# A transformer front on one core: input loaded token-major, turned and scaled by a matmul with a diagonal, and a new order of transfers and small work

## The chip, the cores and the metric

The kernel runs on one core of a Trainium2 chip. The metric is device time in microseconds of one execution, lower is better. The engines named here: TensorE (PE, matmuls), VectorE (DVE), ScalarE (ACT), GpSimd (POOL), SyncE (SP, which issues the transfers).

## The reference

Two transformer-like layers in sequence over 512 tokens of width 1024, in float32. The change concerns only the beginning of the first one:

```
mod = silu(c) @ w_ada + b_ada            # 6144 numbers: sh1, sc1, ga1, sh2, sc2, ga2
y   = x * rsqrt(mean(x * x, -1) + EPS)   # a root of each token
xn  = (y * g_mix) * (1 + sc1) + sh1
proj = xn @ w_in + b_in                  # q, k, v, index q, index k, index weights, RNN inputs, gates
score = sum_h wi[q,h] * relu(qi . ki)    # for the choice of the 128 best keys of a query
```

From `proj` come an attention over the chosen keys, a gated linear recurrence (RG-LRU) behind a causal convolution, a merge, a feed-forward part, and then a second layer with 16 meta tokens ahead. The recurrence needs `softplus(-lam)` of 1024 numbers, called the factor below.

## The kernel before

Everything is held with features on the partitions: `H` is [128, 8, 528], eight chunks of 128 features by 16 meta tokens and 512 tokens. Weights come in 560 units of 512 KB, each [128, 8, 128], through two buffers `raw`. GpSimd splits each unit into a high and a low part (`Whi`, `Wlo`, L422 to L428); TensorE multiplies the split input by the split weight with three matmuls for each chunk (L443 to L445), 24 for a unit over 512 tokens. A split waits until TensorE has left the slot (`half_done`, `unit_done`), and SyncE loads a unit when the unit two before it has been split (`weights_ready`).

The engines run one list of instructions each and are ordered by semaphores alone. The front, in the order of its lists:

SyncE loads c, part of the constants, two small tables for the bias rows (`REL`, `OH`), x already transposed into `H` in four transfers of 512 KB, the meta tokens, the vectors `V`; then the rows of `w_ada`, 512 KB each, into eight slots `AW`: 16 rows in the order of `FRONT_ROWS` (scale and shift of each chunk), and 24 more. A row waits until the row eight before it has been used (`ada_done`). `UNIT_BEHIND_ROW` and `AHEAD` say behind which rows the weight units 0 to 11 are issued; a unit that waits holds everything behind it.

ScalarE squares the chunks of x (L966), TensorE sums them over the partitions with a matrix of 1/1024 (L525), ScalarE makes the roots `RSTP`. VectorE reduces each row against silu(c) to one number per partition (L1391), multiplies x by the roots two chunks at a time (`spread`, L1395), and ScalarE applies scale and shift twice, to the high half `XAhi` (L982) and to the plain product `NTP` in PSUM (L985); VectorE takes the difference as `XAlo` (`low(k)`, L1400). Units 0 to 3 are multiplied chunk by chunk as these arrive (`BLOCKS`): the groups hold 1, 3, 4, 4, 5, 5, 5 and 5 blocks of three matmuls. VectorE takes the first four pairs of rows before the first spread.

Behind the front VectorE's list holds the 16 rows L1369 (`modulation`), with `bound_ratio` (four small instructions) after eight of them; then `WI`, the index weights (L1475, `wi_ready`), for which the score matmul n == 3 waits; then 24 score sums with the last eight rows between them; then the factor, 28 small instructions (`factor_begin`, `factor_terms`, `factor_end`, L1435 to L1467); then the products for the meta tokens (L1539) and the taps of the first convolution (L1547), for which the first gate matmuls (L586) wait. TensorE runs units 4, 5 and 6, the transposes for `WI`, six scores (L557) behind each of units 6 to 9, and the recurrence units from 10 on, with the first gates behind unit 13. Some matmuls on zeros (L514, L531) fill TensorE's time at the start.

Of the kernel before, what the change touches and what calls it, by code (L numbers as in the profile page):

```python
# [75 lines left out]
UNIT_BEHIND_ROW = {3: 0, 5: 1, 8: 2, 10: 3}  # L76
AHEAD = {2: 4, 4: 5, 14: 6, 17: 7, 19: 8, 21: 9, 23: 10, 24: 11}
# [43 lines left out]
def build(nc, xT, metaT, vecs, rel, onehot, consts, crow, ada, gatew, units, scratch, out):  # L121
    with ExitStack() as ctx:
        def sb(name, shape, dt=F32, frame=ctx):
            return frame.enter_context(nc.sbuf_tensor(name, shape, dt))

        def sem(name):
            return ctx.enter_context(nc.semaphore(name))
# [34 lines left out]
        sb("fill", [P, 40])  # L162
# [5 lines left out]
        RSTP = A45[:, 0:S]  # L168
        NTP = [A45[:, 0:512] if k in (5, 7) else A45[:, 512:1024] for k in range(KC)]
# [5 lines left out]
        with ExitStack() as f:  # L175
# [6 lines left out]
            XS = RG8  # L182
# [78 lines left out]
        v_in, xs_ready, meta_copied = sem("v_in"), sem("xs_ready"), sem("meta_copied")  # L261
# [88 lines left out]
        def _(sp):  # L350
            sp.dma_start(CR[0:1, :], crow.rearrange("(o d) -> o d", o=1)).then_inc(c_in, 16)
            sp.dma_start(CON[:, 0:C_ONE], consts[:, 0:C_ONE]).then_inc(mean_in, 16)
            sp.dma_start(REL[:, :], rel).then_inc(small_in, 16)
            sp.dma_start(OH[:, :], onehot).then_inc(small_in, 16)
            for j in range(KC // 2):
                sp.dma_start(H[:, 2 * j:2 * j + 2, META:T], xT[:, 2 * j:2 * j + 2, :]).then_inc(x_in[j], 16)
                if j == 0:
                    sp.dma_start(H[:, :, 0:META], metaT).then_inc(meta_in, 16)
                if j == 1:
                    sp.dma_start(V[:, :], vecs).then_inc(v_in, 16)  # L360
# [79 lines left out]
        def _(pe):  # L440
# [89 lines left out]
            for _ in range(11):  # L530
                pe.matmul(gp[0][:, 0:HALF], SQS[:, 0:P], SQS[:, 0:HALF], start=True, stop=True)  # L531
# [3 lines left out]
            for j, blocks in enumerate(BLOCKS):  # L535
                pe.wait_ge(xn_ready, j + 1)
                for u, k in blocks:
                    if (u, k) == (1, 0):
                        pe.wait_ge(rb_copied, 1)
                    if (u, k) == (2, 0):  # L540
                        pe.wait_ge(meta_copied, 1)
                    split_wait(u, k)
                    mm = three(gp[u % 2][:, (u // 2) * 512:(u // 2) * 512 + S], u, k, XAhi[:, k, :], XAlo[:, k, :], k == 0, k == KC - 1)
                    if k == KC // 2 - 1:
                        mm.then_inc(half_done, 1)
                    if k == KC - 1:
                        mm.then_inc(unit_done, 1)
# [362 lines left out]
        def _(act):  # L910
# [51 lines left out]
            for k in range(KC):  # L962
                act.wait_ge(x_in[k // 2], 16)
                if k >= 2:
                    act.wait_ge(stat_mm, k - 1)
                act.activation(sq[:, k % 2, 0:S], H[:, k, META:T], ACT.Square).then_inc(sq_ready, 1)  # L966
                if k == KC // 2:
                    act.wait_ge(meta_in, 16)
                    act.activation(MSQ[:, :, :], H[:, :, 0:META], ACT.Square).then_inc(meta_sq, 1)
            act.wait_ge(stat_mm, KC)  # L970
            inverse_root(RSTP, RSTP, EPSC, rstd_ready)
# [289 lines left out]
        def _(dve):  # L1261
# [123 lines left out]
            dve.wait_ge(silu_c, 1)  # L1385

            def rows(k):
                for n, c in ((2 * k, KC + k), (2 * k + 1, k)):
                    w = AW[n % ADA_SLOTS]
                    dve.wait_ge(ada_in[n % ADA_SLOTS], 16 * (n // ADA_SLOTS + 1))  # L1390
                    dve.tensor_tensor_reduce(w[:, :], w[:, :], CSP, 1.0, 0.0, ALU.mult, ALU.add, MOD[:, c:c + 1]).then_inc(ada_done, 1)  # L1391
                dve.drain().then_inc(mod_ready, 1)
# [15 lines left out]
            spread(2)
            low(1)
            spread(3)  # L1410
            low(2)
            rows(4)
            low(3)
            rows(5)
            low(4)
            rows(6)
            rows(7)
            for k in (5, 6, 7):
                low(k)
# [51 lines left out]
            modulation(ADA_FIRST + 8, ADA_FIRST + 16)  # L1471
# [172 lines left out]
            dve.drain()  # L1644
            residual(1, U_OUT, 1, 2 * KC)
# [329 lines left out]
```

## Time and profile before

| | us |
|---|---|
| median of 3 runs | 1746.54 (1746.23 to 1747.31) |
| the profiled execution, its own time | 1745.25 |
| its span in the profile | 1743.3 |
| TensorE busy | 1714.8 (98%) |
| GpSimd busy | 1473.8 (85%) |
| VectorE busy | 1080.4 (62%) |
| ScalarE busy | 530.5 (30%) |

Times in the trace are microseconds from the start of the span; durations marked ns are nanoseconds. Busy time of TensorE is that of its pipelined matmuls, so neighbours overlap; the granted clock (PEclk) is a share of full speed, where 1.00 is 2.4 GHz and 0.50 is 1.2 GHz. An idle time stands in brackets with the instruction that ended it.

### The profile page before, as it was taken

The numbers are of one execution on the slowest core, as the hardware profiler recorded it, in microseconds if no ns is written. First come the engines' busy times: TensorE is split into PE (matmuls) and PEld (weight loads), VectorE is DVE, ScalarE is ACT, GpSimd is POOL, SyncE is SP. The second block draws the span as 40 slices with busy tenths as digits, with TensorE's granted clock in tenths as the row PEclk, the third lists the DMA queues.
The fourth block names the chain that finished last, engine by engine and source line by source line (L and its number), as shares of the span: only waits on it lengthen the run. The fifth ranks groups of instructions, "written<-read, shape, count | busy, mean of one in ns | idle before, by whom it ended". The sixth has DMA issues, their size and how long they took to land.

```text
span 1743.3 us, 35057 instructions
## 1 busy us (share of the span) xinstructions
PE 1714.8 (98%) x12334; PEld 1531.0 (88%) x12334; DVE 1080.4 (62%) x1682; ACT 530.5 (30%) x801; POOL 1473.8 (85%) x2245
## 2 busy tenths in 40 slices
PE   8999999999999999999999999999999999999998
PEld 5667776678899999988899999999999999999887
DVE  6788998845566767622678676876685455555102
ACT  5336664311221211100443444444343211111001
POOL 4577996578999999999689888988897999999885
PEclk8999999999999999999999999999999999999999
DMA  9942332232332332333222222222232332333332
GB/s 341 394 143 82 94 100 89 93 107 87 98 96 86 94 95 86 97 109 108 62 86 84 86 73 86 86 76 83 80 92 73 97 93 88 96 96 96 97 108 97
DMA packets 55384, 184.54 MB, mean 106 GB/s; under 512 B 6721, under 2 KB 9953, under 8 KB 55298
## 3 DMA queue, kind: packets, MB, share of 16 engines
q1 hardware_dynamic: 52066, 177.53, 32.2%
q10 hardware_dynamic: 3232, 5.77, 0.9%
q8 instruction: 66, 1.08, 0.3%
q14 instruction: 20, 0.16, 0.0%
HBM read 178.56 MB, written 4.72 MB: 105 GB/s over the span
## 4 chain that ended last, share of the span: by engine, by line
PE 90%; DVE 5%; DMA 1%; ACT 1%; DVEq 1%; issue 1%; SPq 1%; ACTq 0%; POOL 0%; POOLq 0%
PE gp L443 28%; PE gp L444 28%; PE gp L445 28%; DMA AW<-ada 1%; PE A L586 1%; DMA raw<-units 1%; PE A L804 1%; PE A L619 1%; PE gp L645 1%; PE A L855 1%; PE A L637 0%; DVE AW L1391 0%; PE A L799 0%; PE A L857 0%; PE A L847 0%
## 5 line engine op out<-in xcount | busy, mean ns | idle before, releaser
L426 POOL TENSOR_TENSOR Wlo<-raw,Whi 128x256 fp32r<-128x256 f32 x1120 | 981.0, 896 | 46.7
L443 PE MATMUL gp<-XNhi,Whi 128*128 128x258 f32 (+3 forms) x2736 | 840.1, 307 | 8.1 <-DVE XNlo L1400 3.2
L444 PE MATMUL gp<-XNlo,Whi 128*128 128x258 f32 (+3 forms) x2736 | 829.4, 303 | 0.0
L445 PE MATMUL gp<-XNhi,Wlo 128*128 128x258 f32 (+3 forms) x2736 | 827.0, 302 | 0.0
L443 PEld LDWEIGHTS gp<-XNhi,Whi 128*128 128x128 f32 x2736 | 515.4, 188 | 41.4 <-issue 11.9
L444 PEld LDWEIGHTS gp<-XNlo,Whi 128*128 128x128 f32 x2736 | 515.6, 188 | 23.5 <-issue 2.4
L445 PEld LDWEIGHTS gp<-XNhi,Wlo 128*128 128x128 f32 x2736 | 515.0, 188 | 22.0
L422 POOL TENSOR_TENSOR probe<-raw 1x1 f32<-1x1 f32 x560 | 180.6, 323 | 203.9 <-PE gp L445 140.2
L423 POOL TENSOR_SCALAR Whi<-raw 128x512 fp32r<-128x512 f32 x560 | 342.5, 612 | 0.0
L443 PE MATMUL gp<-AChi,Whi 128*128 128x512 f32 (+1 forms) x374 | 141.0, 377 | 0.0
L444 PE MATMUL gp<-AClo,Whi 128*128 128x512 f32 (+1 forms) x374 | 140.8, 377 | 0.0
L445 PE MATMUL gp<-AChi,Wlo 128*128 128x512 f32 (+1 forms) x374 | 140.8, 377 | 0.0
L443 PEld LDWEIGHTS gp<-AChi,Whi 128*128 128x128 f32 x374 | 70.4, 188 | 13.0
L445 PEld LDWEIGHTS gp<-AChi,Wlo 128*128 128x128 f32 x374 | 70.4, 188 | 13.0
L444 PEld LDWEIGHTS gp<-AClo,Whi 128*128 128x128 f32 x374 | 70.4, 188 | 12.7
L930 ACT ACTIVATE sq<-H 128x512 f32<-128x512 f32 (+1 forms) x24 | 15.2, 633 | 180.2 <-DVE H L1305 147.7
L1303 DVE TENSOR_TENSOR H<-gp,H 128x514 f32<-128x514 f32 (+2 forms) x15 | 10.4, 693 | 94.4 <-PE gp L445 94.2
L1242 ACT ACTIVATE ffn_val<-ZZ,V 128x512 f32<-128x512 f32 x22 | 18.0, 817 | 154.6 <-DVEq L1843 154.6
L1846 DVE SCALAR_TENSOR_TENSOR ffn_val<-ZZ,V,ffn_val 128x512 f32<-128x512 f32 x44 | 43.9, 998 | 31.6 <-ACT ffn_val L1242 27.9
L1305 DVE SCALAR_TENSOR_TENSOR H<-gp,MOD,H 128x512 f32<-128x512 f32 (+1 forms) x16 | 12.0, 751 | 82.6 <-PE gp L445 82.2
L1723 DVE TENSOR_TENSOR DD<-h_G 128x640 f32<-128x640 f32 x48 | 56.1, 1182 | 5.7 <-issue 1.2
L1741 DVE TENSOR_TENSOR XX<-h_k,EE 128x320 f32<-128x320 f32 x48 | 49.4, 1028 | 0.0
(334 smaller groups left out, 2234.9 us busy)
## 6 DMA issues: line engine op xcount, KB each, us to landing
raw<-units SPq DMA_DIRECT2D x280, 512.0 KB, 3.5
AW<-ada SPq DMA_DIRECT2D x40, 512.0 KB, 8.5
AWL<-ada SPq DMA_DIRECT2D x8, 512.0 KB, 3.6
bias_rows<-RB ACTq DMA_DIRECT2D x1, 2560.0 KB, 19.8
H<-xT SPq DMA_DIRECT2D x4, 512.0 KB, 6.6
BIAS<-bias_rows ACTq DMA_DIRECT2D x1, 2048.0 KB, 7.8
out<-H SPq DMA_DIRECT2D x8, 256.0 KB, 2.2
WG<-gatew ACTq DMA_DIRECT2D x8, 128.0 KB, 2.0
```

The costliest lines, as they stand in the source:

```text
L422: pool.tensor_tensor(probe[0:1, 0:1], src[0:1, c0:c0 + 1], src[0:1, c0:c0 + 1], ALU.add)
L423: pool.tensor_scalar(hi[:, c0:c1], src[:, c0:c1], 1.0, 1.0, ALU.mult, ALU.mult).then_inc(hi_made, 1)
L426: ins = pool.tensor_tensor(lo[:, c:c + UNIT // 4], src[:, c:c + UNIT // 4], hi[:, c:c + UNIT // 4].bitcast(F32), ALU.subtract)
L443: pe.matmul(dst, Whi[s][:, k, :], rhi, start=start, stop=False)
L444: pe.matmul(dst, Whi[s][:, k, :], rlo, start=False, stop=False)
L445: return pe.matmul(dst, Wlo[s][:, k, :], rhi, start=False, stop=stop)
L586: pe.matmul(A45[:, r * 512:(r + 1) * 512], WG[:, r * P:(r + 1) * P], XC[b % 2][:, :], start=True, stop=True).then_inc(gate_mm, 1)
L619: pe.matmul(A45[:, g * 512:g * 512 + (i + 1) * P], Q[g * HD:(g + 1) * HD, r * 2 + e, i * P:(i + 1) * P], K[g * HD:(g + 1) * HD, 0:(i + 1) ...
L1242: act.activation(YV[:, :], ZZ[:, 0, 2:2 + S], ACT.Identity, bias=fw(3), scale=fw(2)).then_inc(ya_first, 1)
L1723: dve.tensor_tensor(DD[:, l % 2, :].rearrange("p (j t) -> p j t", t=2 * b), g, g[:, :, b - 1:b].to_broadcast([P, TP // (2 * b), 2 * b]), A ...
L1741: dve.tensor_tensor(x[:, :, 0, :], k[:, :, 0, :], e[:, :, 0, :], ALU.mult)
L1846: dve.scalar_tensor_tensor(YV[:, :], ZZ[:, 0, tap:tap + S], V[:, bass.ds(VEC["ffn2"] + i * 4 + tap, 1)], YV[:, :], ALU.mult, ALU.add)
```

## The change

x is loaded twice: first with tokens on the partitions, four transfers of 512 KB into `XK`, and once more transposed into `H`, in one transfer of 2 MB behind the last row of `w_ada`, for the residual much later. The two small tables go behind x. VectorE sums the squares of a token along its row, one reduction for each 128 tokens (`TOK`); ScalarE makes 512 roots as [128, 4]; VectorE scales the identity by them (`DIAG`). A matmul of a 128x128 piece of `XK` with the diagonal turns the piece and scales it (`turned(k)`: four for each chunk, into the PSUM bank `XSP`), in place of the sums over partitions and of `spread`. ScalarE's two passes read `XSP`, and `NTP` is one bank instead of two. VectorE's rows and low halves alternate: row 2k, low k-1, row 2k+1. Units 0 and 1 are issued two rows earlier, units 6 to 11 one to six rows earlier. The factor moves from behind the scores to between the 16 modulation rows ahead of `WI`.

```diff
-UNIT_BEHIND_ROW = {3: 0, 5: 1, 8: 2, 10: 3}
-AHEAD = {2: 4, 4: 5, 14: 6, 17: 7, 19: 8, 21: 9, 23: 10, 24: 11}
+UNIT_BEHIND_ROW = {1: 0, 3: 1, 8: 2, 10: 3}
+AHEAD = {2: 4, 4: 5, 8: 6, 11: 7, 14: 8, 17: 9, 20: 10, 23: 11}
...
+        XSP, NTP = A45[:, 0:S], A45[:, S:2 * S]
+        DIAG = sq[:, 0, 0:S].rearrange("p (t n) -> p t n", t=QT)
...
+            XK = RG8[:, :, :].rearrange("p k n -> p (k n)").rearrange("p (t d) -> p t d", t=QT)
... SyncE
+            for t in range(QT):
+                sp.dma_start(XK[:, t, :], xrow[t, :, :]).then_inc(x_in[t], 16)
+                if t == 0:
+                    sp.dma_start(H[:, :, 0:META], metaT).then_inc(meta_in, 16)
+                if t == 2:
+                    sp.dma_start(V[:, :], vecs).then_inc(v_in, 16)
             sp.dma_start(REL[:, :], rel).then_inc(small_in, 16)
             sp.dma_start(OH[:, :], onehot).then_inc(small_in, 16)
...
+            sp.dma_start(H[:, :, META:T], xT).then_inc(h_in, 16)
             load_units(U_RNN + 2, U_ROUT)
... TensorE
-            for k in range(KC):
-                pe.wait_ge(sq_ready, k + 1)
-                pe.matmul(RSTP, mean, sq[:, k % 2, 0:S], start=(k == 0), stop=(k == KC - 1)).then_inc(stat_mm, 1)
...
-            for _ in range(11):
+            def turned(k):
+                if k:
+                    pe.wait_ge(nt_ready, k)
+                for t in range(QT):
+                    mm = pe.matmul(XSP[:, t * P:(t + 1) * P], XK[:, t, k * P:(k + 1) * P], DIAG[:, t, :], start=True, stop=True)
+                mm.then_inc(xs_mm, 1)
+            for _ in range(4):
+                pe.matmul(gp[0][:, 0:HALF], SQS[:, 0:P], SQS[:, 0:HALF], start=True, stop=True)
+            pe.wait_ge(diag_ready, 1)
+            turned(0)
+            for _ in range(6):
                 pe.matmul(gp[0][:, 0:HALF], SQS[:, 0:P], SQS[:, 0:HALF], start=True, stop=True)
...
             for j, blocks in enumerate(BLOCKS):
+                if j + 1 < KC:
+                    turned(j + 1)
                 pe.wait_ge(xn_ready, j + 1)
... ScalarE
+            act.wait_ge(tok_sums, 1)
+            act.activation(TOK[:, 1, :], TOK[:, 0, :], ACT.Ln, bias=EPSC, scale=1.0 / D)
+            act.drain()
+            act.activation(TOK[:, 1, :], TOK[:, 1, :], ACT.Exp, scale=-0.5).then_inc(rstd_ready, 1)
...
-                act.wait_ge(xs_ready, k // 2 + 1 if k != 5 else KC // 2)
-                act.activation(XAhi[:, k, :], XS[:, k, :], ACT.Identity, bias=SHB[:, k:k + 1], scale=AB1[:, k:k + 1]).then_inc(xhi_ready, 1)
+                act.wait_ge(xs_mm, k + 1)
+                act.activation(XAhi[:, k, :], XSP, ACT.Identity, bias=SHB[:, k:k + 1], scale=AB1[:, k:k + 1]).then_inc(xhi_ready, 1)
                 if k:
-                    act.wait_ge(xn_ready, k if k < 5 else k - 1)
-                act.activation(NTP[k], XS[:, k, :], ACT.Identity, bias=SHB[:, k:k + 1], scale=AB1[:, k:k + 1]).then_inc(nt_ready, 1)
+                    act.wait_ge(xn_ready, k)
+                act.activation(NTP, XSP, ACT.Identity, bias=SHB[:, k:k + 1], scale=AB1[:, k:k + 1]).then_inc(nt_ready, 1)
... VectorE
+            for t in range(QT):
+                dve.wait_ge(x_in[t], 16)
+                dve.tensor_tensor_reduce(AWL[0][:, :], XK[:, t, :], XK[:, t, :], 1.0, 0.0, ALU.mult, ALU.add, TOK[:, 0, t:t + 1])
+                dve.drain()
+            dve.memset(probe[0:1, 29:30], 0.0).then_inc(tok_sums, 1)
...
+            dve.wait_ge(rstd_ready, 1)
+            for t in range(QT):
+                ins = dve.tensor_scalar(DIAG[:, t, :], ident, TOK[:, 1, t:t + 1], None, ALU.mult)
+            ins.then_inc(diag_ready, 1)
+            dve.wait_ge(silu_c, 1)
+            row(0)
+            row(1)
+            for k in range(1, KC):
+                row(2 * k)
+                low(k - 1)
+                row(2 * k + 1)
+            low(KC - 1)
...
             modulation(ADA_FIRST, ADA_FIRST + 8)
             bound_ratio()
-            modulation(ADA_FIRST + 8, ADA_FIRST + 16)
+            factor_begin()
+            modulation(ADA_FIRST + 8, ADA_FIRST + 11)
+            factor_terms(13, 11, 9, 7)
+            modulation(ADA_FIRST + 11, ADA_FIRST + 14)
+            factor_terms(5, 3, 1)
+            factor_end()
+            modulation(ADA_FIRST + 14, ADA_FIRST + 16)
 
             dve.wait_ge(con_in, 16)
             dve.wait_ge(wi_mm, 1)
... behind the scores
-            factor_begin()
-            factor_terms(13, 11, 9, 7, 5, 3, 1)
-            factor_end()
             dve.wait_ge(meta_rstd, 1)
...
+            dve.wait_ge(h_in, 16)
             residual(1, U_OUT, 1, 2 * KC)
```

## Rows read from the trace of the kernel before

**Rows 1.** The page, busy time of TensorE, its share and instructions.
```profile
PE 1714.8 (98%) x12334; PEld 1531.0 (88%) x12334; DVE 1080.4 (62%) x1682; ACT 530.5 (30%) x801; POOL 1473.8 (85%) x2245
```
**Rows 2.** Waits of TensorE, 28 to 150 us: total us, times, longest.
```profile
PE gp L443 <- DVE XNlo L1400: 3.2, 3, 1.2
PE gp L443 <- POOL Wlo L426: 3.1, 1, 3.1
```
**Rows 3.** Windows: length; busy us by engine; granted clock, transfers' share, GB/s.
```profile
13.00:19.00 6.00, 5.89 (x7) 2.43 (x8) 3.98 (x7) 2.14 (x5) 0.00 (x0) 0.50 1.02 417
68.00:72.00 4.00, 0.90 (x4) 0.48 (x3) 2.62 (x5) 0.69 (x1) 2.58 (x6) 1.00 1.02 416
88.00:104.00 16.00, 16.00 (x69) 10.76 (x68) 14.20 (x23) 6.76 (x14) 10.76 (x19) 1.00 0.28 98
131.00:136.00 5.00, 5.00 (x13) 2.94 (x12) 3.65 (x6) 3.52 (x5) 0.05 (x1) 0.66 0.43 134
```
**Rows 4.** Timeline of TensorE: start us, us, instruction, pieces, idle before.
```profile
8.77 1.02 PE L521 MATMUL gp<-OH,REL 32*128 32x512 f32 x2
...
23.44 1.85 PE L528 MATMUL gp<-MSQ,CON 128*128 128x16 f32 x16
25.14 5.00 PE L531 MATMUL gp<-SQS 128*128 128x256 f32 x22
31.30 0.47 PE L443 MATMUL gp<-XNhi,Whi 128*128 128x512 f32 x1 [1.16 <-DVE XNlo L1400]
...
126.83 0.39 PE L443 MATMUL gp<-XNhi,Whi 128*128 128x512 f32 x1
...
127.28 0.39 PE L445 MATMUL gp<-XNhi,Wlo 128*128 128x512 f32 x1
130.72 2.71 PE L586 MATMUL A<-rnn_xc,WG 128*128 128x512 f32 x4 [3.05 <-DVE rnn_xc L1547]
```
**Rows 5.** The chain that ended last, the first matmul of unit 7.
```profile
79.84 0.43 PE gp L443
```
**Rows 6.** Timeline of VectorE: front rows, low half, later rows, WI, factor, meta.
```profile
36.20 1.22 DVE L1391 CUSTOM_DVE_ANT_0 AW<-AW,A 128x1024 f32<-128x1024 f32 x1
...
37.56 0.69 DVE L1400 TENSOR_TENSOR XNlo<-A,XNhi 128x512 fp32r<-128x512 f32 x1
...
49.03 1.21 DVE L1369 CUSTOM_DVE_ANT_0 AW<-AW,A 128x1024 f32<-128x1024 f32 x1
...
58.16 0.16 DVE L1423 TENSOR_TENSOR LAM<-LAM 128x8 f32<-128x8 f32 x1
...
77.88 0.19 DVE L1475 TENSOR_SCALAR WI<-gp 128x32 f32<-128x32 f32 x1 [4.90 <-PE gp L569]
...
110.98 0.51 DVE L1435 TENSOR_SCALAR LAM<-LAM 128x8 f32<-128x8 f32 x1
...
124.55 2.79 DVE L1539 SCALAR_TENSOR_TENSOR MSQ<-H,V,MRS 128x16 f32<-128x16 f32 x8
```
**Rows 7.** Timeline of ScalarE: scale of one chunk, and its second pass.
```profile
37.51 0.39 ACT L978 ACTIVATE AB<-MOD,GB,V 128x1 f32<-128x1 f32 x1 [1.04 <-DVEq L1392]
...
38.87 0.76 ACT L985 ACTIVATE A<-RG,SHB,AB 128x512 f32<-128x512 f32 x1
```
**Rows 8.** Tile H, 0 to 30 us: issues of x (first, last start), landing.
```profile
L356 SPq DMA_DIRECT2D H<-xT x4: 426/452/648, 2.5 to 5.4; - x4
...
DMA to landing us min/median/max: 3.7/6.1/8.0
```
**Rows 9.** Tile LAM, 50 to 130 us: duration ns min/median/max.
```profile
L1448 DVE TENSOR_TENSOR LAM<-LAM x7: 166/616/737, 113.8 to 119.7; 128x8 f32<-128x8 f32 x7
```
**Rows 10.** Timeline of SyncE, the issue of unit 6.
```profile
57.40 0.33 SPq L370 DMA_DIRECT2D raw<-units  x1
```
**Rows 11.** Transfers, 50 to 60 us: packets, MB, share of 16 engines.
```profile
q1 hardware_dynamic: 660, 2.43, 61.1%
q10 hardware_dynamic: 643, 1.65, 41.0%
```

More of the change, by code:

```diff
@@ L118, in region, with build @@
     return 0 if n <= 512 else 512 - spans(n)[0][1]
-def build(nc, xT, metaT, vecs, rel, onehot, consts, crow, ada, gatew, units, scratch, out):
+def build(nc, xT, xrow, metaT, vecs, rel, onehot, consts, crow, ada, gatew, units, scratch, out):
     with ExitStack() as ctx:
@@ L161, in build @@
         GB1 = sb("GB1", [P, KC])
-        sb("fill", [P, 40])
+        TOK = sb("TOK", [P, 2, QT])
+        sb("fill", [P, 32])
         ident, ones, tri, mean, head_mean = [CON[:, c:c + P] for c in (C_ID, C_ONE, C_TRI, C_MEAN, C_HMEAN)]
@@ L167, in build @@
         CSP = A67[:, 0:D]
-        RSTP = A45[:, 0:S]
-        NTP = [A45[:, 0:512] if k in (5, 7) else A45[:, 512:1024] for k in range(KC)]
+        XSP, NTP = A45[:, 0:S], A45[:, S:2 * S]
+        DIAG = sq[:, 0, 0:S].rearrange("p (t n) -> p t n", t=QT)
         SCP = (A45[:, 0:512], A45[:, 512:1024], gp[1][:, 512:1024], gp[0][:, 512:1024])
@@ L260, in build @@
                                                         sem("meta_in"))
[L261 removed]
+        v_in, xs_mm, meta_copied, h_in = sem("v_in"), sem("xs_mm"), sem("meta_copied"), sem("h_in")
+        diag_ready, tok_sums = sem("diag_ready"), sem("tok_sums")
         eps_ready, row_ready, row_mm = sem("eps_ready"), sem("row_ready"), sem("row_mm")
@@ L352, in _ @@
             sp.dma_start(CON[:, 0:C_ONE], consts[:, 0:C_ONE]).then_inc(mean_in, 16)
+            for t in range(QT):
[4 more added lines that the diff above has]
+                    sp.dma_start(V[:, :], vecs).then_inc(v_in, 16)
             sp.dma_start(REL[:, :], rel).then_inc(small_in, 16)
             sp.dma_start(OH[:, :], onehot).then_inc(small_in, 16)
[L355 to L360, printed above, removed]
             def load_units(first, last):
@@ L961, in _ @@
             act.wait_ge(eps_ready, 1)
[L962 to L971, printed above, removed]
+            act.wait_ge(meta_in, 16)
+            act.activation(MSQ[:, :, :], H[:, :, 0:META], ACT.Square).then_inc(meta_sq, 1)
+            act.wait_ge(tok_sums, 1)
+            act.activation(TOK[:, 1, :], TOK[:, 0, :], ACT.Ln, bias=EPSC, scale=1.0 / D)
+            act.drain()
+            act.activation(TOK[:, 1, :], TOK[:, 1, :], ACT.Exp, scale=-0.5).then_inc(rstd_ready, 1)
             act.wait_ge(meta_mm, 1)
@@ L1384, in _ @@
             dve.scalar_tensor_tensor(GB1[:, :], vec("b_ada", KC, KC), 1.0, vec("g_mix", 0, KC), ALU.add, ALU.mult)
[L1385 to L1392, printed above, removed]
@@ L1394, in spread, with row @@
-            def spread(j):
-                dve.tensor_tensor(XS[:, 2 * j:2 * j + 2, :], H[:, 2 * j:2 * j + 2, META:T],
-                                  RSTP.rearrange("p (o n) -> p o n", o=1).to_broadcast([P, 2, S]), ALU.mult).then_inc(xs_ready, 1)
+            def row(n):
+                c, w = FRONT_ROWS[n], AW[n % ADA_SLOTS]
+                dve.wait_ge(ada_in[n % ADA_SLOTS], 16 * (n // ADA_SLOTS + 1))
+                dve.tensor_tensor_reduce(w[:, :], w[:, :], CSP, 1.0, 0.0, ALU.mult, ALU.add, MOD[:, c:c + 1]).then_inc(ada_done, 1)
+                if n % 2:
+                    dve.drain().then_inc(mod_ready, 1)
@@ L1398, in low @@
             def low(k):
                 dve.wait_ge(nt_ready, k + 1)
-                dve.tensor_tensor(XAlo[:, k, :], NTP[k], XAhi[:, k, :].bitcast(F32), ALU.subtract).then_inc(xn_ready, 1)
-            for k in range(KC // 2):
-                rows(k)
+                dve.tensor_tensor(XAlo[:, k, :], NTP, XAhi[:, k, :].bitcast(F32), ALU.subtract).then_inc(xn_ready, 1)
+            dve.wait_ge(mean_in, 16)
             dve.wait_ge(rstd_ready, 1)
-            spread(0)
-            spread(1)
-            low(0)
@@ L1408, in _ @@
[L1408 to L1419, printed above, removed]
+            for t in range(QT):
[4 more added lines that the diff above has]
+            row(1)
@@ L1953 @@
         "xT": a["x"][0].T.reshape(KC, P, S).swapaxes(0, 1),
+        "xrow": a["x"][0].reshape(QT, P, D),
         "metaT": a["meta_tokens_2"].T.reshape(KC, P, META).swapaxes(0, 1),
```

3 lines of the change are left out of this document (2 added, 1 removed).

## Prediction

> **What bounds the kernel now.** I read the page first: TensorE is busy 1714.8 of 1743.3 us [rows 1], so a change pays only through TensorE's gaps or its clock. The list of TensorE's waits, taken over the stretch the diff touches, gives them: 3.2 us in three waits for the low halves of the normed input (L1400), 3.1 us for one weight unit, 3.05 us at the first recurrence gate for the convolution on VectorE [rows 2, 4]. After those TensorE is never again released by this front. The windows add the clock: 0.50 over 13 to 19 us, after TensorE had waited for the first squares, and 0.66 over 131 to 136 us behind the gate's wait, though the 3.1 us wait inside 68 to 72 us left it at 1.00 [rows 3]. Last I read TensorE's, VectorE's and ScalarE's timelines side by side [rows 4 to 7]. There the reader is to see that VectorE runs one list without a branch: front rows, low halves, 16 more modulation rows, then the index weights WI at 77.88 us [rows 6]. TensorE's fourth score matmul waits for WI (wi_ready). In the old kernel VectorE reaches WI with time in hand and TensorE is the late one.
>
> **The change, step by step.** *The start.* The old first block begins at 31.30 us [rows 4], after eight modulation rows and the spreads. The new one needs the four token sums, the diagonal, two rows and one turned block. The last of the old x transfers landed 8.0 us after its issue near 5.4 [rows 8], so at 13.4; the new last one has 96 KB less before it: 12.5 to 13.4, I take 13.2. The last token sum is a reduction of the rows' shape (1.22 us and its accumulator read, [rows 6]): 14.5. A small Ln and Exp, and four 128x128 products that no row shows (below, 128x8 at 0.17 us [rows 9]; above, a 512-wide one at 0.69 [rows 6]): 16.0, within 15.2 and 17.6. Two rows at 1.14 us, the pitch of the eight between 49.03 and 58.16 [rows 6], end at 18.4.
>
> TensorE is later than that. Its bias matmul now waits for the small tables, which are queued behind x and land at 13.4; it ran at 8.8 before [rows 4]. Then come 1.2 us of bias, 1.7 of meta statistics (16 pieces, 1.85 with the tail), four fillers of 0.455 (22 pieces in 5.00) [rows 4] and the turned block. The turned block is eight 128-column passes; between the pace of the meta pieces (0.116 us) and that of the 256-column fillers (0.227) they take 0.9 to 1.8 us, I take 1.0. Together 5.7 us at 2.4 GHz. TensorE has idled more than 3 us by then, and in the row of 13 to 19 us it then worked at 1.2 GHz for six us [rows 3]; behind the gate it was 3.4 us (5 us at a mean of 0.66). So 3.4 to 6 us at half pace add 1.7 to 3 us: turned(0) is done at 20.9 to 22.2, I take 21.5. ScalarE's two passes follow (1.4 us), and low(0) ends at 23.5. The first block starts some 7.5 us earlier than before.
>
> *The chain of the eight blocks.* Here the new order hides a ring. row(2k+1) stands behind low(k-1) in VectorE's list, low(k-1) waits for ScalarE's second pass, and that pass waits for the row before. One turn: row start to ScalarE's start 36.20 to 37.51, ScalarE to the end of the second pass 37.51 to 38.87 + 0.76, then low, 0.65 from start to next start [rows 6, 7]: 1.31 + 2.12 + 0.65 = 4.08 us. Reading PSUM instead of SBUF may move it to 3.9 or 4.2. The old order took its rows four ahead. Seven turns make 28.6 us: low(7) ends at 52.0 (49.5 to 53.5). The old list left low(7) at 49.03 [rows 6]. So VectorE leaves the front 3 us later, although TensorE enters it 7.5 us earlier. The seven turned blocks inside (7 us) lie in TensorE's waits for that ring: five blocks of three matmuls at 0.23 (126.83 to 127.28 is two, [rows 4]) and one turn are 4.4 us against 4.08.
>
> *From there to WI.* VectorE still has 16 rows: 16 x 1.14 = 18.3 us. The moved factor work now stands before WI. It was 28 small instructions in the 13.57 us from 110.98 to 124.55 [rows 6], 0.485 us each, and with the four of the bound ratio there are 32. A single one takes 0.166 to 0.737 us [rows 9]; at the least, with the gap behind it, 0.25. So 8.0 to 15.5 us; I take 0.40 us each, 12.8 us, because TensorE's wait fills the weight slots and GpSimd then rests part of the time. The Trainium skill weighs on this price: SBUF — State Buffer, section "Who interferes with whom", says that a VectorE instruction with two SBUF inputs and a GpSimd one that reads SBUF exclude each other for the whole instruction. By it the 0.25 us holds wherever GpSimd rests, and with GpSimd at rest for half of this stretch the sum would be some 1.5 us smaller; the spread in rows 9 agrees with it, but no row shows these instructions beside an idle GpSimd.
>
> Transfers: unit 6 is asked for when unit 4 is split, which waits for unit 0. That was at 57.40 [rows 10] and is now near 55. Up to the row of the last block of three stand eight transfers of 0.52 MB and the constants of 0.75 MB, 4.95 MB. While the bias rows go out the queue moves 2.43 MB in 10 us beside their 1.65 [rows 11], afterwards the whole 0.41 MB a us. The bias rows, 2.6 MB from 52 on at 0.165, last until 68: 2.8 MB by then, the rest by 73.3, landed near 75. VectorE wants that row 13 rows and 17 small instructions after 52.0, near 73.6: 1.2 us of waiting (0 to 4).
>
> WI: 52.0 + 18.3 + 12.8 + 1.2 = 84.3 us, against 77.88.
>
> *TensorE behind WI.* It ends the blocks near 55 and three units at 72, and waits some 12 us. After WI three scores take 1.5 us (from WI to unit 7 it was 77.88 to 79.84 [rows 5, 6], part of it overlapped). The fall of the clock costs 1.7 us (rows of 131 to 136) to 3 (13 to 19), I take 2.0. Unit 7 in effect starts at 87.8, 8.0 us later than 79.84. The early gains, the 3.1 us wait for unit 6 among them, end in this wait. The Trainium skill speaks to the 2.0: TensorE: Matmul & The Clock Gate, Part 1, calls the lower level the default, which only activity lifts. By it this wait must pay it, and without it the sum would be 2.0 us smaller; rows 3 show both outcomes after 3 us, and none after 12.
>
> *The gate.* Behind the scores no factor work is left. VectorE needs 33.1 us from WI to the end of the scores (77.88 to 110.98) and 6.2 for the meta products and the taps (124.55 to the gate at 130.72) [rows 4, 6]: ready at 123.6. TensorE comes at 127.67 + 8.0. The wait of 3.05 us [rows 4] is gone, and the 1.7 us of clock behind it: -4.75 us.
>
> *What costs nothing.* The second load of x, 2 MB or 5.1 us of all queues, goes out near 97 us by my estimate, where transfers use 0.28 of the engines [rows 3]; the residual that needs it is far behind. Uncovered it would cost unit 12 up to 5 us. Longer rows in the x transfer, one buffer instead of two for the second pass: inside the ring's spread.
>
> Sum: +8.0 - 4.75 = +3.2 us. The profiled execution took 1745.25 us (span 1743.3), the median of the runs is 1.29 above it: 1746.54 + 3.2 = 1749.7 us. A time within 0.2%, 3.5 us, can't be told from no change here.
>
> **The rivals.** Everything hangs on when VectorE reaches WI. Break-even is 84.3 - 3.2 = 81.1 us, and each us there is a us of time.
>
> Faster: VectorE is through by 77.6 or before. That needs small instructions near 0.25 us (8.0 us) and the ring near 3.9 us from an early start (low(7) at 49.5): 75.8, hence -5.3 us, 1741.3. For it speaks the shortest of the small instructions; against it the mean of 0.485 over 28. Chance 0.12.
>
> No change: WI between 77.6 and 81.1, when one of the two is cheap: -3.5 to 0, 1745. Chance 0.14.
>
> Much slower: WI after 87.5, because rows arrive late behind the bias rows and the constants (4 us instead of 1.2) and the small instructions keep 0.485 (15.5): 89.8, +8.7 us, 1755. For it speak the 1.65 MB that share the queue; against it that the queue is empty when unit 6 is asked for. Chance 0.11.
>
> The extra x load delays unit 12: +3 to +5 us on the forecast, 1754. Against it the 0.28. Chance 0.03.
>
> **How the numbers follow.** The forecast, WI between 81.1 and 87.5, has 0.60; a little over half of it lies under 84.6, within 3.5 us of no change. Faster 0.12; same 0.14 + 0.33 = 0.47; slower 0.27 + 0.14 = 0.41. The range reaches to WI at 78.6 and 90: 1744 to 1755.5, which leaves out most of the faster case and the tail of the slow one. The forecast's own range is 1746.5 to 1753.
>
> **What would show it.** Right: first block near 23.5, low(7) near 52, one TensorE wait of about 12 us for WI near 72 to 84, clock 0.50 behind it, no wait at the first gate. Wrong at the ring: turns of the low halves well under 4 us. Wrong at the price: the 32 small instructions under 10 us. Wrong altogether: TensorE waits less than 5 us before WI, or VectorE waits for rows longer than 4 us.

## The result, and the profile after

Median of 15 runs 1749.99 us (1748.83 to 1751.58), beside 1746.23 us for the kernel before (15 runs of the same series): ratio 1.0025, 95% interval 1.0017 to 1.0032. The change makes the kernel slower by 0.25%. The profiled execution took 1748.93 us, its span is 1747.1.

TensorE's waits after, from 28 to 150 us (total us, times, longest); they stand against [rows 2] and the wait of the gate in [rows 4]:

```profile
PE gp L571 <- DVE WI L1488: 9.9, 1, 9.9
PE A L535 <- ACT A L995: 2.1, 2, 1.3
```

One wait of 9.9 us for WI, and two of together 2.1 us for ScalarE at the turned blocks, have taken the place of the old ones. The windows after, in the columns of [rows 3]:

```profile
13.00:19.00 6.00, 6.00 (x23) 5.07 (x22) 4.65 (x13) 1.35 (x5) 3.41 (x7) 0.50 1.02 408
...
76.00:84.00 8.00, 0.00 (x0) 0.00 (x0) 6.94 (x20) 0.00 (x0) 3.53 (x6) 0.51 1.03 409
84.00:90.00 6.00, 5.51 (x15) 3.96 (x16) 5.35 (x12) 1.54 (x4) 0.00 (x0) 0.51 0.54 213
...
131.00:136.00 5.00, 5.00 (x23) 4.13 (x22) 0.00 (x0) 0.24 (x2) 3.97 (x7) 1.00 0.39 119
```

In the 76 to 84 us row TensorE does nothing, VectorE is busy 6.94 of 8 us; in the next TensorE works again, at a clock of 0.51. Behind the gate (131 to 136) the clock is now 1.00 where it was 0.66. TensorE's timeline after, against [rows 4]:

```profile
11.83 2.04 PE L524 MATMUL gp<-OH,REL 32*128 32x512 f32 x2 [3.40 <-DMA OH<-onehot]
13.66 0.63 PE L525 MATMUL gp<-OH,REL 32*128 32x128 f32 x2
14.22 3.60 PE L528 MATMUL gp<-MSQ,CON 128*128 128x16 f32 x16
17.66 3.76 PE L539 MATMUL gp<-SQS 128*128 128x256 f32 x8
21.21 1.22 PE L535 MATMUL A<-sq,RG 128*128 128x128 f32 x8
...
25.67 0.47 PE L446 MATMUL gp<-XNhi,Whi 128*128 128x512 f32 x1
...
73.13 0.41 PE L583 MATMUL gp<-CON,WIT 8*128 8x8 f32 x4
...
84.49 0.79 PE L571 MATMUL gp<-KI,QI 64*128 64x256 f32 x1 [9.89 <-DVE WI L1488]
...
86.49 0.79 PE L446 MATMUL gp<-XNhi,Whi 128*128 128x512 f32 x1
...
135.79 1.88 PE L600 MATMUL A<-rnn_xc,WG 128*128 128x512 f32 x4
```

The first weight block starts 5.6 us earlier than before, unit 7 (86.49) 6.65 us later than in [rows 5], the first gate 5.1 us later. VectorE's timeline after, against [rows 6]:

```profile
23.92 0.69 DVE L1412 TENSOR_TENSOR XNlo<-A,XNhi 128x512 fp32r<-128x512 f32 x1 [5.96 <-ACT A L995]
24.53 1.21 DVE L1406 CUSTOM_DVE_ANT_0 AW<-AW,A 128x1024 f32<-128x1024 f32 x1
...
25.93 1.22 DVE L1406 CUSTOM_DVE_ANT_0 AW<-AW,A 128x1024 f32<-128x1024 f32 x1 [0.18 <-issue]
...
27.93 0.69 DVE L1412 TENSOR_TENSOR XNlo<-A,XNhi 128x512 fp32r<-128x512 f32 x1 [0.77 <-ACT A L995]
...
51.94 0.69 DVE L1412 TENSOR_TENSOR XNlo<-A,XNhi 128x512 fp32r<-128x512 f32 x1 [2.17 <-ACT A L995]
52.55 1.21 DVE L1386 CUSTOM_DVE_ANT_0 AW<-AW,A 128x1024 f32<-128x1024 f32 x1
```

Here is the ring: low, row, row, and 0.77 us of idle time, until ScalarE is done, before the next low; from 23.92 to 51.94 it is seven turns of 4.00 us. ScalarE in its turn stands idle until VectorE has done the row:

```profile
25.84 0.39 ACT L988 ACTIVATE AB<-MOD,GB,V 128x1 f32<-128x1 f32 x1 [1.95 <-DVEq L1408]
```

WI follows at 84.25, 6.4 us later than before.

### The profile page after: what moved, and what is told of

Same layout as the page of the kernel before. It is cut to its first block, busy times and chain, and to the rows that moved or that the text cites. A ratio compares the mean times of both kernels' runs of the same rounds, so it can differ in the third digit from the quotient of the medians.

```text
span 1747.1 us, 35152 instructions
## 1 busy us (share of the span) xinstructions
PE 1715.4 (98%) x12380; PEld 1536.9 (88%) x12380; DVE 1079.8 (62%) x1693; ACT 524.5 (30%) x793; POOL 1472.7 (84%) x2245
## 4 chain that ended last, share of the span: by engine, by line
PE 92%; DVE 4%; ACT 2%; DVEq 1%; issue 0%; DMA 0%; SPq 0%; ACTq 0%
PE gp L446 29%; PE gp L447 28%; PE gp L448 28%; DVE AW L1386 1%; PE A L600 1%; PE A L818 1%; PE A L633 1%; PE gp L659 1%; PE A L869 1%; PE A L651 0%; DVEq L1408 0%; PE A L813 0%; PE A L871 0%; PE A L861 0%; ACT XNhi L992 0%
## 5 line engine op out<-in xcount | busy, mean ns | idle before, releaser
L447 PEld LDWEIGHTS gp<-AClo,Whi 128*128 128x128 f32 x374 | 70.4, 188 | 12.8
L448 PEld LDWEIGHTS gp<-AChi,Wlo 128*128 128x128 f32 x374 | 70.4, 188 | 12.8
## 6 DMA issues: line engine op xcount, KB each, us to landing
bias_rows<-RB ACTq DMA_DIRECT2D x1, 2560.0 KB, 13.4
```

Source lines behind the costliest of these rows:

```text
L447: pe.matmul(dst, Whi[s][:, k, :], rlo, start=False, stop=False)
L448: return pe.matmul(dst, Wlo[s][:, k, :], rhi, start=False, stop=stop)
```

## The experiments

The change has three edits that can be taken apart: the start, the queue's two tables, and the place of the factor. Seven of their eight combinations were timed (the kernel before is one, old start with new queue and new factor is left out), each beside runs of the kernel before:

| start | queue | factor | ratio to before, 95% | median us |
|---|---|---|---|---|
| old | new | old | 1.0007 (0.9998 to 1.0017) | 1746.68 |
| old | old | new | 0.9985 (0.9976 to 0.9994) | 1743.28 |
| new | old | old | 1.0024 (1.0015 to 1.0033) | 1750.07 |
| new | new | old | 1.0020 (1.0011 to 1.0029) | 1748.68 |
| new | old | new | 0.9998 (0.9989 to 1.0007) | 1745.59 |
| new | new | new | 1.0025 (1.0017 to 1.0032) | 1749.99 |

So the start alone costs 0.24%, and 0.13% where the queue or the factor is new as well; there the intervals overlap. The factor's new place gains with the old queue (0.15% at the old start, 0.26% at the new one) and nothing that can be told with the new queue. And the new queue takes 0.27% where the other two are in. Its two tables were moved together in these runs; they don't tell the one from the other. Times of different profiles are compared below from a common event, low(0) or score(3) (the score matmul n == 3, which waits for WI), because x lands up to 1.5 us apart from one execution to the next.

**The factor back at its old place; start and queue stay new.**

```diff
             bound_ratio()
-            factor_begin()
-            modulation(ADA_FIRST + 8, ADA_FIRST + 11)
-            factor_terms(13, 11, 9, 7)
...
+            modulation(ADA_FIRST + 8, ADA_FIRST + 16)
...
             dve.memset(XR[:, 0:3], 0.0).then_inc(xr_pad, 1)
+            factor_begin()
+            factor_terms(13, 11, 9, 7, 5, 3, 1)
+            factor_end()
```

> The changed kernel with the factor's 28 small instructions back at their old place behind the scores; the new start and the new queue stay. Theory (VectorE's list up to WI sets the time): without them WI comes as soon as TensorE has turned its input, near 74 us in place of 84.25; TensorE's wait of 9.9 us at score(3) and its half clock are gone, unit 7 starts near 76.6 (86.5 in the changed kernel, 79.8 in the kernel before). VectorE then has the factor behind the scores again, so a wait of 2 to 4 us at the first gate returns. Sum: 3.5 us below the kernel before (2 to 4.5), about 1742.7. Rival (the new start or the second load of x is what costs): unit 7 is not ahead of 79.8, and the time stays within 1 us of the changed kernel, 1749 to 1751.

1748.68 us. The expected gain of 3.5 us over the kernel before did not come: WI stands at 80.01, not near 74. VectorE's longest waits there, 50 to 85 us, were for rows:

```profile
DVE AW L1386 <- DMA AW<-ada: 5.9, 3, 3.1
```

SyncE's timeline in the same run shows why (start us, us; L372 is a unit, L376 a group of rows):

```profile
57.93 0.33 SPq L372 DMA_DIRECT2D raw<-units  x1
58.30 2.72 SPq L376 DMA_DIRECT2D AW<-ada  x3
62.43 0.33 SPq L372 DMA_DIRECT2D raw<-units  x1
...
68.98 0.33 SPq L372 DMA_DIRECT2D raw<-units  x1
69.35 1.39 SPq L376 DMA_DIRECT2D AW<-ada  x3
74.03 0.33 SPq L372 DMA_DIRECT2D raw<-units  x1
```

In the new queue three rows go out behind each unit from 6 on, and a unit's load waits until GpSimd has freed its buffer. The last two rows ahead of WI stand behind unit 8: they are asked for from 69.35 on, when that unit has gone out at 68.98, and VectorE, which has waited for them, begins the first at 77.58. In the changed kernel the factor's instructions lie over these waits, so none shows there.

**The kernel before with the factor alone moved** (the diff above the other way round, on the old start and queue).

> The kernel before with only the factor moved ahead of WI, dealt out between the rows as in the changed kernel; start and queue are the old ones. Theory: 28 small instructions of 0.40 us lie ahead of WI, so WI moves from 77.9 to about 89, TensorE waits some 11 us more at score(3) and falls to half clock, and the gate's wait of 3.05 us and the 1.7 us of clock behind it go away: unit 7 starts 11 us later, about 89 to 91; time 5 to 8 us above the kernel before, 1751 to 1754. Rival (the factor ahead of WI is hidden, because WI waits for something else there): within 1 us of the kernel before less the gate's 4.7 us, 1741 to 1743.

1743.28 us, a gain of 1.9 us: outside both ranges, but close to the rival's. In the kernel before VectorE waited 4.9 us for TensorE ahead of WI [rows 6], and in four places from 63 to 71 us for rows:

```profile
DVE AW L1369 <- DMA AW<-ada: 3.7, 4, 1.3
```

The moved instructions fill those 8.6 us, WI comes at 79.83, TensorE waits 1.7 us for it, and the gate's wait is gone. The expectation had put the factor's whole length on the path, without that cover.

**The new start alone** (factor back as in the first run, and the queue's tables as before):

```diff
-UNIT_BEHIND_ROW = {1: 0, 3: 1, 8: 2, 10: 3}
-AHEAD = {2: 4, 4: 5, 8: 6, 11: 7, 14: 8, 17: 9, 20: 10, 23: 11}
+UNIT_BEHIND_ROW = {3: 0, 5: 1, 8: 2, 10: 3}
+AHEAD = {2: 4, 4: 5, 14: 6, 17: 7, 19: 8, 21: 9, 23: 10, 24: 11}
```

> The new start alone: factor back behind the scores and the queue's tables as before. With the factor back alone, rows waited 5.9 us in three places for transfers that stood in the queue behind units 7 to 9, which waited for GpSimd, and WI came at 80.0. Theory: the old queue sends the first 14 rows ahead of unit 6, these waits shrink to 1 to 4 us as in the kernel before (3.7), WI comes at 75 to 77.5, TensorE's wait at score(3) shrinks from 4.2 to 0 to 2 and its clock stays up; the wait of some 3 us at the first gate stays: 1742 to 1745, that is 3 to 6 us below the run with the factor back alone. Rival (the ring of the new start is the price, whatever the queue): WI not before 79, within 1 us of the run with the factor back.

1750.07 us: rows wait only 3.5 us, as the theory says, but the time is no better. TensorE's waits, 28 to 150 us, and SyncE's issue of unit 6:

```profile
PE gp L446 <- POOL Wlo L429: 6.9, 1, 6.9
PE A L600 <- DVE rnn_xc L1554: 2.8, 1, 2.8
...
61.09 0.48 SPq L372 DMA_DIRECT2D raw<-units  x1
```

The bound moved to unit 6. Its load stands behind row 14, whose slot is free when VectorE has used the row eight before; VectorE is late by the ring, so the load goes out at 61.09, where it was 57.40 [rows 10], and TensorE, which has left unit 5 at 69 in both kernels, waits 6.9 us in place of 3.1 [rows 2]. This is how the ring costs even where WI has time.

**The old queue in the changed kernel** (the two lines above, start and factor as changed).

> The changed kernel with the two tables of the queue (which unit's load stands behind which row's) as they were before; start and factor as changed. Theory: with the factor's instructions between the rows no row waits for a transfer in the changed kernel, so the new queue neither costs nor gives anything there: within 0.7 us of the changed kernel, WI within 0.7 us of 84.2. Rival (units loaded earlier pay later: unit 6 to 11 earlier by up to 6 us): 1 to 3 us slower than the changed kernel. Second rival (the new queue is the price): 2 us or more faster.

1745.59 us, 4.4 us under the changed kernel: the second rival, not the theory. TensorE's waits, 28 to 150 us:

```profile
PE gp L446 <- POOL Wlo L429: 5.6, 1, 5.6
...
PE gp L571 <- DVE WI L1488: 0.3, 1, 0.3
```

VectorE's timeline, two of the factor's terms and two later ones:

```profile
69.52 0.17 DVE L1457 TENSOR_SCALAR LAM<-LAM 128x8 f32<-128x8 f32 x1
69.77 0.17 DVE L1455 TENSOR_TENSOR LAM<-LAM 128x8 f32<-128x8 f32 x1
...
75.34 0.66 DVE L1457 TENSOR_SCALAR LAM<-LAM 128x8 f32<-128x8 f32 x1
76.07 0.73 DVE L1455 TENSOR_TENSOR LAM<-LAM 128x8 f32<-128x8 f32 x1
```

GpSimd's timeline, the end of one unit's split and the start of the next:

```profile
61.50 1.43 POOL L429 TENSOR_TENSOR Wlo<-raw,Whi 128x256 fp32r<-128x256 f32 x2
72.98 0.18 POOL L425 TENSOR_TENSOR probe<-raw 1x1 f32<-1x1 f32 x1 [10.05 <-DMA raw<-units]
73.14 0.61 POOL L426 TENSOR_SCALAR Whi<-raw 128x512 fp32r<-128x512 f32 x1
```

And two windows:

```profile
72.00:78.00 6.00, 2.62 (x6) 2.15 (x7) 5.61 (x12) 0.00 (x0) 4.32 (x8) 0.50 1.03 414
84.00:90.00 6.00, 5.67 (x27) 4.46 (x27) 5.41 (x10) 1.86 (x6) 5.75 (x10) 1.00 0.79 307
```

Score(3) in this run, then in the run with the second load of x moved (below):

```profile
84.39 0.48 PE L571 MATMUL gp<-KI,QI 64*128 64x256 f32 x1 [0.33 <-DVE WI L1488]
...
85.36 0.79 PE L571 MATMUL gp<-KI,QI 64*128 64x256 f32 x1 [9.59 <-DVE WI L1488]
```

Two things are to be seen. First, TensorE's idle time is cut in two: 5.6 us lie ahead of unit 6, and the half clock behind them (72 to 78) falls on unit 6, which WI leaves time for; at score(3) the clock is 1.00 (84 to 90). From score(3) to the first gate it is 48.79 us here and 51.30 in the changed kernel: 2.5 us. Part of that differs from one profile to the next: in the run with the second load of x moved, whose wait for WI is 9.59 us, the same stretch took 50.44 us. There the clock was back at 1.00 from 89 us on, and in the changed kernel, where score(3) stands 0.87 us earlier, only from 90 on. By that run the half clock costs 1.7 us. Second, GpSimd has no unit to split from 62.9 to 73.0, and in that time the factor's instructions take 0.17 us; beside its splits they take 0.66 and 0.73. From low(7) to WI it is 30.2 us in place of 32.3: 2.1 us. Together 3.8 to 4.6 us; 4.4 were measured.

**The kernel before with the new queue alone** (the same two lines the other way).

> The kernel before with only the two tables of the queue as in the changed kernel; old start, factor behind the scores. Theory from the runs so far (the new queue ties rows 9 to 16 to the pace at which GpSimd frees buffers for units 6 to 9, so WI can't come before some 79 us, and moves TensorE's wait from ahead of unit 6 to the scores): no wait of 3.1 us for unit 6, instead one of 3 to 5 us for WI at score(3) with the clock at 0.50 behind it; 1 to 3 us above the kernel before. Rival (loads of units ahead of time are a gain in themselves): the 3.1 us are saved and nothing takes their place, 2 to 4 us below the kernel before.

1746.68 us, not told apart from before. The wait for unit 6 shrank to 0.9 us, a wait of 4.0 us for WI came in its place, with the clock at 0.50 from 80 to 84, and rows waited 11.1 us. The mechanism is as expected, the sum is at the bottom of what was expected.

**Rows one pair further ahead** (the ring broken, else as changed):

```diff
-            row(0)
-            row(1)
-            for k in range(1, KC):
-                row(2 * k)
-                low(k - 1)
-                row(2 * k + 1)
-            low(KC - 1)
+            for n in range(4):
+                row(n)
+            for k in range(KC):
+                low(k)
+                if k + 2 < KC:
+                    row(2 * k + 4)
+                    row(2 * k + 5)
```

> The changed kernel with VectorE's rows one pair further ahead: four rows before low(0), and behind each low(k) the two rows of part k+2. Nothing else. Theory (the ring of 4.00 us a turn: row, coefficients, scaled read, subtraction): with the rows out of the ring its turns shrink to what TensorE needs (turned block 1.05 us and up to five weight blocks of 0.68 us), low(7) starts near 50 in place of 51.9, WI and the end come 2 us earlier (1 to 2.5), about 1747.5 to 1749. Rival (TensorE's turned blocks are the limit in the turns already): low(7) stays within 0.5 us of 51.9 and the time within 0.5 us of the changed kernel. A second rival, from the run with the factor put back: the rows' loads stand in the queue behind units that wait for GpSimd, so rows wait for their transfers and WI moves less than low(7) does.

1746.40 us, 3.6 us under the changed kernel, more than the 1 to 2.5 expected. VectorE's timeline:

```profile
25.45 0.69 DVE L1412 TENSOR_TENSOR XNlo<-A,XNhi 128x512 fp32r<-128x512 f32 x1 [5.12 <-ACT A L995]
...
32.05 0.69 DVE L1412 TENSOR_TENSOR XNlo<-A,XNhi 128x512 fp32r<-128x512 f32 x1
35.15 0.69 DVE L1412 TENSOR_TENSOR XNlo<-A,XNhi 128x512 fp32r<-128x512 f32 x1
...
46.29 0.69 DVE L1412 TENSOR_TENSOR XNlo<-A,XNhi 128x512 fp32r<-128x512 f32 x1 [1.40 <-ACT A L995]
50.67 0.69 DVE L1412 TENSOR_TENSOR XNlo<-A,XNhi 128x512 fp32r<-128x512 f32 x1 [3.69 <-ACT A L995]
```

Turns of 3.10 us in the middle, where VectorE itself is the limit, and of 4.38 in the last two, where five weight blocks and a turned one fill TensorE. From low(0) to low(7) it is 25.2 us in place of 28.0, to WI 56.7 in place of 60.3.

**The small tables on ScalarE's queue at the start** (else as changed):

```diff
-            sp.dma_start(REL[:, :], rel).then_inc(small_in, 16)
-            sp.dma_start(OH[:, :], onehot).then_inc(small_in, 16)
...
+            act.dma_start(REL[:, :], rel).then_inc(small_in, 16)
+            act.dma_start(OH[:, :], onehot).then_inc(small_in, 16)
             act.wait_ge(row_mm, 1)
```

> The changed kernel with the two small tables loaded from ScalarE's queue at the very start in place of SyncE's behind x; nothing else. Theory (the late tables hold TensorE, and with it the first turned block and the whole ring): TensorE's wait of 2.7 to 4.2 us for them goes, turned(0) follows the diagonal at once, low(0) comes 3 to 4.5 us earlier (near 21), the ring keeps its 4.00 us a turn, so low(7) and WI come as much earlier unless rows wait for transfers: 2 to 4 us below the changed kernel, 1746 to 1748. Rival (weights or rows are not there yet that early, so that the ring waits for them): low(7) moves under 1.5 us and the time under 1.5 us.

1748.01 us, ratio 1.0012 (1.0003 to 1.0021), which overlaps the changed kernel's interval a little. The wait for the tables is gone, but one of 2.7 us for ScalarE's squares of the meta tokens stands in its place, so low(0) is at 23.40 and not near 21; the ring keeps 4.00 us. The gain of some 2 us lies at the low end of what was expected; low(0) moved less than that, for a reason neither side named.

**The second load of x moved behind the recurrence.**

```diff
-            sp.dma_start(H[:, :, META:T], xT).then_inc(h_in, 16)
...
             load_late(1)
+            sp.dma_start(H[:, :, META:T], xT).then_inc(h_in, 16)
```

> The changed kernel with the second load of x (2 MB into H) issued behind the whole recurrence, next to the late rows, in place of near 98 us. Theory: at 98 us this transfer has nobody waiting; the time stays within 0.5 us of the changed kernel, and unit 12's load is issued some us earlier without use. Rival (the transfer holds up the units' loads and is the price of the change): 2 to 4 us below the changed kernel, back at the time of the kernel before.

1749.97 us, ratio 1.0029 (1.0017 to 1.0041): no difference from the changed kernel. Where the second load stands, it costs nothing that can be told.

**Matmuls on zeros in TensorE's wait**, first 38, then 20:

```diff
                 if n == 3:
+                    for _ in range(38):
+                        pe.matmul(gp[1][:, 0:HALF], SQS[:, 0:P], SQS[:, 0:HALF], start=True, stop=True)
                     pe.wait_ge(wi_ready, 1)
```

> The changed kernel with 38 small matmuls on zeros into a free half bank put into TensorE's wait for WI (some 9 us at the full clock), nothing else. Theory: WI is as late as before, 84.2, but the granted clock stays at 1.00 through the wait, so unit 6's scores and unit 7, which ran at half clock from 84.5 to 89.6, give back about 2.5 us (1.5 to 3). Rival (the clock costs nothing there because VectorE and ScalarE set the pace of the scores behind WI): within 0.5 us of the changed kernel.

> As the run with 38 matmuls on zeros in TensorE's wait, with 20: one took 0.44 us there, not the 0.23 that the first sizing went by, so 38 of them (16.7 us) held score(3) back by 6.5 us behind WI. 20 take 8.8 us and end before WI. Theory: the granted clock stays at 1.00 through the wait, WI is where it was, and the 5 us at half clock behind it give back 2.5 us (1.5 to 3): 1746.5 to 1748.5. Rival (VectorE and ScalarE set the pace behind WI): within 0.5 us of the changed kernel.

With 38: 1753.95 us. They took 16.67 us, twice what they were sized for, so score(3) ran 6.5 us after WI, where it runs 0.24 us after it in the changed kernel. The windows of that run:

```profile
76.00:92.00 16.00, 16.00 (x77) 13.82 (x74) 11.10 (x29) 1.04 (x3) 4.31 (x8) 1.00 0.87 343
92.00:98.00 6.00, 6.00 (x28) 4.55 (x27) 3.41 (x6) 1.04 (x3) 0.65 (x2) 1.00 0.00 0
```

The clock is 1.00 throughout, and from score(3) to the gate it is 48.80 us: the same 2.5 us less as with the old queue. 6.3 later less 2.5 is 3.8 us above the changed kernel; 4.0 were measured. With 20: 1747.40 us, ratio 1.0010 (1.0001 to 1.0019), 2.6 us under the changed kernel by the medians, with intervals that overlap a little. Its profile doesn't bear out that size: TensorE rested 1.53 us between the last of them and WI, and the clock fell behind that:

```profile
86.00:92.00 6.00, 5.89 (x20) 4.55 (x21) 5.41 (x12) 1.53 (x4) 0.14 (x1) 0.72 0.49 197
```

Score(3) to gate is 50.42 us, no shorter than in the run with the second load moved, which has no such matmuls (50.44). But the profiled execution took 1749.69 us, and eight of the eleven took 1746.32 to 1748.14. Whether the clock stayed up in those, none of which was profiled, stays open, and with it what the 2.6 us are.

**A version made from these runs:** tables on ScalarE's queue, rows ahead, `UNIT_BEHIND_ROW` new and `AHEAD` old, and the factor dealt out to where VectorE has time (ScalarE's three exponentials for it move ahead too, behind the roots):

```diff
             for n in range(4):
                 row(n)
+            bound_ratio()
...
+            modulation(ADA_FIRST, ADA_FIRST + 10)
+            factor_begin()
+            modulation(ADA_FIRST + 10, ADA_FIRST + 13)
+            factor_terms(13, 11)
+            modulation(ADA_FIRST + 13, ADA_FIRST + 16)
...
+            factor_terms(9, 7, 5, 3, 1)
+            factor_end()
```

> A version made from what the runs showed: the new start with the tables on ScalarE's queue and with the rows one pair further ahead (no ring), units 0 and 1 asked for early as in the changed kernel, units from 6 on behind the rows as in the kernel before, the bound ratio in VectorE's idle time ahead of low(0), nine of the factor's instructions between the last rows and the other nineteen behind the scores. Theory: low(0) near 21, low(7) near 46, WI near 70 to 73, and unit 6 asked for soon enough; TensorE's waits between 28 and 135 us together under 4 us, unit 7 at 72 to 76 (86.5 in the changed kernel, 79.8 before), gate wait under 2 us: 4 to 8 us below the kernel before, 1737 to 1741. Rival (the transfers, whose engines are busy through this stretch, set the pace of rows and units whatever the order): waits for rows and units of 5 us or more, 0 to 3 us below the kernel before.

1739.10 us, ratio 0.9963 (0.9950 to 0.9977). The time is within what was expected, though low(0) is at 23.42 and not near 21, WI at 76.70 and not at 70 to 73, and unit 7 at 78.59. VectorE waits 5.6 us for TensorE ahead of WI, and TensorE has waited for one thing, 28 to 150 us:

```profile
PE gp L444 <- POOL Wlo L427: 4.1, 1, 4.1
```

That is unit 6 again, behind row 14. The last run asks for it behind row 10:

```diff
-AHEAD = {2: 4, 4: 5, 14: 6, 17: 7, 19: 8, 21: 9, 23: 10, 24: 11}
+AHEAD = {2: 4, 4: 5, 10: 6, 17: 7, 19: 8, 21: 9, 23: 10, 24: 11}
```

> The version made from the runs, with unit 6 asked for behind row 10 in place of row 14. In that version TensorE still waited 4.1 us for unit 6, whose load was issued at 56.55 and landed at 66.65, behind four more rows, while VectorE waited 5.6 us for TensorE ahead of WI. Theory (the place in the queue decides): the load goes out at 56, its buffer's earliest, but with 2 MB less ahead of it, and lands near 61 to 62, before TensorE wants it near 64.6; rows 11 to 14 come 2 to 3 us later, inside VectorE's 5.6 us; TensorE's wait and its half clock (69 to 72) go: 3 to 5 us below that version, 1734 to 1736. Rival (whatever goes first, rows and units share the same transfer rate): VectorE now waits 5 us or more for rows, WI comes no earlier than 76, within 1 us of that version or slower.

1736.91 us, ratio 0.9947 (0.9933 to 0.9960), 0.5% faster than the kernel before. The load lands at 61.66 as expected, WI comes at 73.67. TensorE's wait for unit 6 is gone; what is left of its waits, 28 to 150 us:

```profile
PE gp L569 <- DVE WI L1485: 2.1, 1, 2.1
```

And VectorE's wait ahead of WI:

```profile
DVE WI L1485 <- DMA CON<-consts: 1.6, 1, 1.6
```

WI now waits for the constants, which are issued behind unit 7. Over the version before it the gain is 2.2 us by the medians, less than the 3 to 5 expected, and the two intervals overlap.

## Why the prediction came out right

It forecast 1749.7 us, at the edge of what can be told from no change; 1749.99 was measured. Its sum of +3.2 us stands against 1748.93 - 1745.25 = +3.7 us between the two profiled executions. The two parts of the sum came out as well: TensorE was ready for the gate 8.1 us later than before (135.79 against 127.67; forecast 8.0), and from there on it gained 4.4 us (forecast 4.75).

*The start.* Later than forecast: turned(0) was done at 22.4 (forecast 21.5), low(0) ended at 24.6 (23.5). x, the tables and the diagonal came early (the last token sum began at 11.28 us, the tables' matmul at 11.83, forecast 13.4, and the diagonal was there at 14.3, forecast 16.0), but TensorE needed 10.6 us from the bias matmul to the turned block, not 5.7 plus at most 3: nearly all of it ran at half clock. In the seven other profiles with this start and the tables behind x, low(0) begins 1.1 to 2.1 us later still, at 24.98 to 26.04.

*The ring.* 4.00 us a turn against 4.08. low(7) ended at 52.55 against 52.0. The run with the rows ahead shows that it is a ring and what it costs: 2.8 us to low(7), 3.6 us of time. This is the step on which the forecast's sign rests, and the runs bear it out: the start alone makes the kernel slower by 0.24%, and with the ring broken the changed kernel is level with the kernel before (1.0001).

*From there to WI.* 32 small instructions took 13.3 us (31.7 from low(7) to WI less 16 rows of 1.15), forecast 12.8. The transfers' wait was 0, forecast 1.2. WI at 84.25, forecast 84.3: small errors that cancel in this execution, which is luck. In the three other profiles with the same lists of VectorE and SyncE up to there, WI stands at 85.11, 85.88 and 86.66; all four lie inside the case that was forecast, 81.1 to 87.5. Two side sums of the forecast don't come out of their own figures: 16 small instructions at 0.25 and 16 at 0.485 are 11.8 us, 1.0 and not 1.5 under 12.8, and from 55 to 68 us the queue moves 3.2 MB at 0.243 a us and not 2.8, which would have brought the awaited row nearly in time.

*TensorE behind WI.* The wait was 9.9 us, forecast 12, since TensorE came out of unit 6 at 73 and not 72 and did the first three scores before it stopped. The half clock cost 1.7 to 2.5 us, forecast 2.0. The rule of TensorE: Matmul & The Clock Gate, Part 1, in the Trainium skill, that the lower level is the default, agrees with this wait: 0.51 behind it. *The gate's* wait is gone, as forecast, and comes back (3.1 and 2.8 us) in the two runs with the new start and the factor at its old place. *The second load* is free, as forecast.

*What the prediction did not see.* It gave the new queue one term, rows that arrive late, and that was nil; nothing in it says that the queue is worth 4.4 us in this kernel. With the old queue the same ring and the same factor leave the kernel level with the one before (0.9998), so the sign rests on the queue as much as on the ring. The forecast held without that, since it took its price of a small instruction (0.40 us) as a mean over GpSimd busy and at rest (of the 32, 14 started beside a split and took 0.20 to 0.75 us, 18 beside a resting GpSimd and took 0.16 to 0.20), and put the half clock behind WI. Both follow from the new queue: with the old one GpSimd rests for ten microseconds of this stretch, and the half clock falls where it is free. The Trainium skill, SBUF — State Buffer, section "Who interferes with whom", says that VectorE and GpSimd lock each other out for a whole instruction at the ports that they share; the trace agrees for both kinds of small instruction, TENSOR_TENSOR and TENSOR_SCALAR: 0.17 us without and 0.66 to 0.73 beside a GpSimd whose instructions last 0.61 to 0.72. That "each us of WI is a us of time" held in the run with the rows ahead (3.6 us of WI from low(0), 3.6 of time), and failed with the old queue, where 2.1 us of WI went with 4.4 of time: the clock's part depends on where TensorE stands still, not on WI alone.

## What to carry to other kernels

An engine's list without branches is a schedule: before an edit puts instructions on it, count the waits already in it (8.6 us here), because work laid over these is free and work put into a ring is paid once a turn. A queue's order can be worth as much as the work itself (4.4 us here): a load that waits for a buffer holds everything behind it, and which of two loads goes first decides at which place an engine stands still. Where some standing still can't be avoided, put it where the half clock behind it falls on work that has time.

## What was not expected of the hardware

The clock did not follow the length of TensorE's wait. In the kernel before it stayed at 1.00 through 68 to 72 us with a wait of 3.1 us [rows 2, 3]; in the run with 20 matmuls on zeros a wait of 1.53 us, and in the last version one of 2.1 us, were followed by 0.50 while TensorE was at work again (88 to 90 and 76 to 79 us). Nor does it fall at once: in the changed kernel TensorE stopped at 74.6, and the clock was still 1.00 up to 76.

A small VectorE instruction of 128x8 took 0.16 to 0.20 us whenever GpSimd rested and mostly 0.4 to 0.75 beside its splits, in the kernel before, the changed one and three of the runs (the factor alone moved, the old queue, the rows ahead). So its price hangs on when GpSimd has a weight unit to split.
